# Second layer's attention of a six-layer block on one Trainium2 core: the order of its two branches' pairs, of the weight strips and of the compression

## The reference, cut to what matters

```python
kc = compress(k_cmp, cmp_pe[0], cmp_w1[0], cmp_w2[0])      # gelu(blk @ w1) @ w2, 15 blocks of 32 tokens
vc = compress(v_cmp, cmp_pe[1], cmp_w1[1], cmp_w2[1])
p_c = masked_softmax(s_c, m_c)
o_c = jnp.einsum('bgrqn,bngd->bqgrd', p_c.astype(vc.dtype), vc)
o_s = jnp.einsum('bgrqk,bgqkd->bqgrd', p_s.astype(v_g.dtype), v_g)
o_w = jnp.einsum('bgrqk,bkgd->bqgrd', p_w.astype(vw.dtype), vw)
return gc[..., 0:1] * o_c + gc[..., 1:2] * o_s + gc[..., 2:3] * o_w
```

## Time and profile before

| | us |
|---|---|
| median of 3 runs | 3057.65 |
| lowest, highest | 3055.53, 3057.67 |
| the profiled execution's own time | 3057.54 |
| its span, first to last instruction | 3055.70 |
| mean granted TensorE clock in it | 0.983 of full |

### The profile page before, as it was taken

The page is one execution under the profiler, slowest core; times in us unless marked ns, Lnnn a source line. Parts: engine busy times, 40 slices in busy tenths (PEclk is TensorE's granted clock), DMA queues, the critical chain, the costliest instruction groups (busy, mean ns, idle before and its releaser), DMA issues.

```text
span 3055.7 us, 44834 instructions
## 1 busy us (share of the span) xinstructions
PE 2967.5 (97%) x18942; PEld 2663.0 (87%) x18942; DVE 2128.8 (70%) x2549; ACT 1517.6 (50%) x2040; POOL 39.8 (1%) x30
## 2 busy tenths in 40 slices
PE   9999998999999999999999999999999999999999
PEld 8888997888988899888988989989888898898988
DVE  5677776676657766676877876657778778764776
ACT  5543565434654355534544844545454466454543
POOL 0000000000000000000000000000000000000000
PEclk9999998999999999999999999999999999999999
DMA  7355451354444554355554534535546544352453
GB/s 233 125 166 196 143 177 56 126 196 165 153 138 165 194 169 139 111 197 187 184 196 154 167 127 138 152 104 180 185 165 199 179 152 141 126 165 97 164 195 110
DMA packets 381975, 482.47 MB, mean 158 GB/s; under 512 B 33009, under 2 KB 330143, under 8 KB 381776
## 3 DMA queue, kind: packets, MB, share of 16 engines
q1 hardware_dynamic: 380616, 477.22, 47.5%
q0 software_dynamic: 560, 2.13, 0.2%
q10 hardware_dynamic: 600, 0.27, 0.0%
HBM read 478.47 MB, written 1.08 MB: 157 GB/s over the span
## 4 chain that ended last, share of the span: by engine, by line
PE 85%; DVE 9%; ACT 5%; issue 2%; DMA 0%; DVEq 0%; ACTq 0%
PE ps L425 18%; PE ps L427 17%; PE ps L426 17%; PE ps L464 15%; PE ps L465 7%; DVE wl L408 3%; ACT wh L398 2%; PE ps L463 2%; PE ps L462 1%; PE ps L1377 1%; DVE ar L2689 0%; PE ps L1197 0%; DVE ar L1307 0%; PE ps L714 0%; DVE sm L1312 0%
## 5 line engine op out<-in xcount | busy, mean ns | idle before, releaser
L408 DVE TENSOR_TENSOR wl<-raw,wh 128x2048 fp32r<-128x2048 f32 x456 | 1038.4, 2282 | 424.9 <-ACT wh L398 424.8
L398 ACT ACTIVATE wh<-raw 128x2048 fp32r<-128x2048 f32 x456 | 863.1, 1901 | 479.4 <-PE ps L427 240.2
L464 PE MATMUL ps<-ahl,wh 128*128 128x512 f32 x1904 | 684.0, 398 | 0.0
L425 PE MATMUL ps<-ahl,wh 128*128 128x256 f32 x1928 | 564.5, 293 | 21.6 <-DVE ahl L653 8.7
L426 PE MATMUL ps<-ahl,wh 128*128 128x256 f32 x1928 | 555.0, 288 | 0.0
L427 PE MATMUL ps<-ahl,wl 128*128 128x256 f32 x1928 | 554.5, 288 | 0.0
L465 PE MATMUL ps<-ahl,wl 128*128 128x256 f32 x1904 | 534.7, 281 | 0.0
L464 PEld LDWEIGHTS ps<-ahl,wh 128*128 128x128 f32 x1904 | 358.6, 188 | 76.5
L425 PEld LDWEIGHTS ps<-ahl,wh 128*128 128x128 f32 x1928 | 379.2, 197 | 33.3 <-issue 21.3
L426 PEld LDWEIGHTS ps<-ahl,wh 128*128 128x128 f32 x1928 | 379.7, 197 | 0.3 <-issue 0.2
L427 PEld LDWEIGHTS ps<-ahl,wl 128*128 128x128 f32 x1928 | 379.0, 197 | 0.0
(11 more groups left out here) (409 smaller groups left out, 4087.0 us busy)
## 6 DMA issues: line engine op xcount, KB each, us to landing
raw<-in_ffn_w SPq DMA_DIRECT2D x264, 512.0 KB, 4.2
raw<-in_mlp_w SPq DMA_DIRECT2D x256, 512.0 KB, 4.3
raw<-in_w_in SPq DMA_DIRECT2D x124, 512.0 KB, 4.4
raw<-in_da_w_in SPq DMA_DIRECT2D x48, 512.0 KB, 5.3
raw<-in_ple_gate_w SPq DMA_DIRECT2D x32, 512.0 KB, 4.4
raw<-in_w_ssd_out SPq DMA_DIRECT2D x32, 512.0 KB, 4.3
raw<-in_fox_w_in SPq DMA_DIRECT2D x24, 512.0 KB, 4.6
raw<-in_nsa_w_in SPq DMA_DIRECT2D x20, 512.0 KB, 4.7
```

The source lines that it names most:

```text
L398: nc.scalar.activation(wh[:, slot, 0:sizes[n]], raw[:, slot, 0:sizes[n]], ACT.Copy).then_inc(s_hi, E.adds(s_hi))
L408: nc.vector.tensor_tensor(wl[:, slot, 0:sizes[n]], raw[:, slot, 0:sizes[n]], wh[:, slot, 0:sizes[n]].bitcast(F32), ALU.subtract).then_inc( ...
L425: nc.tensor.matmul(o, wa, xa, start=start, stop=False)
L464: nc.tensor.matmul(o, wa, both, start=start, stop=False)
```

## The change

The 16 pairs go in another order: two of the selected branch, then the same two head pairs of the window branch, and so on by query strips (`nsa_unit`). Window keys are now projected ahead of the loop, window values, queries 1, both compression inputs, queries 2 and queries 3 within turns 0 to 8, by quarters of 12 matmuls before and after a turn's transposes (`NSA_FILL`; all in bank 7, each name waits for the eviction of the one before). Scores are one pair ahead in all turns, each turn does its own values (`deep` is 17 or its default on the other engines, so never used). Gelu moves to turns 6 and 7, the second compression product with all memsets and block copies to turn 9, block scores to 10, mask and sums to 11, block transposes to 12 and 14, products to 13, 14 and 15 (banks 7, 0, 1, 7). Turning the output rows begins after the last values. Values are stored once per group; the block values are copied four times from PSUM, without a copy in SBUF between. Each engine's splits, roundings and loads of strips follow the new order.

```diff
                 else:
-                    dst = orow.rearrange("p q (j c n) -> p c q j n", c=2, n=64)[:, :, :, j % 8, :]
+                    dst = orow.rearrange("p q (j c n) -> p c q j n", c=2, n=64)[:, :, :, unit(j)[0], :]
...
+        NSA_EV = ("q0", "ksel", "gates", "vsel", "kwin", "vwin", "q1", "c0", "c1", "q2", "q3")
+        NSA_FILL = {0: ("vwin", (0, 1), (2, 3)), 1: ("q1", (0,), (1,)), 2: ("q1", (2,), (3,)), 3: ("c0", (0, 1), (2, 3)), 4: ("c1", (0,), (1,)),
+                    5: ("c1", (2,), (3,)), 6: ("q2", (), (0, 1, 2, 3)), 7: ("q3", (0,), (1,)), 8: ("q3", (2,), (3,))}
+        ADDED_BANK = (7, 0, 1, 7)
+
+        def nsa_unit(i):
+
+            return 2 * (i // 4) + i % 2, i % 4 // 2
         nsa_ev = {}
         gah, gal = [view(ar_r, 2048 * v, [P, 16, 60]) for v in range(2)], [view(ar_r, 2048 * v + 1024, [P, 16, 60]) for v in range(2)]
...
+            strip(S)
             for n in range(2):
                 sp_wide(E, d["nsa_cmp_w1"][0, n], 256, 16)
-            for i in range(1, 4):
-                strip(S * i)
-            strip(2048)
-            strip(2304)
+            strip(2 * S)
+            strip(3 * S)
             sp_downs(E, d["nsa_w_out"][0])
...
+
+            def filler(name, part):
+
+
+                if part == 0:
+                    evicted(NSA_EV[NSA_EV.index(name) - 1])
+                    if name == "q2":
+                        E.eng.wait_ge(s_gu, 1)
+                m, h = divmod(part, 2)
+                if name[0] == "c":
+                    n = int(name[1])
+                    if part == 0:
+                        E.eng.wait_ge(s_op, op0 + n + 1)
+                    if h == 0:
+                        held["block"] = pe_block(E, S, DC)
+                    blk, a, b = held["block"]
+                    for k in range(4 * h, 4 * h + 4):
+                        last = mm3(ps[0:60, 7, 0:S], gah[n][:, 8 * m + k], gal[n][:, 8 * m + k], a[:, k, :], b[:, k, :], part == 0 and k == 0, part == 3 and k == DC - 1)
+                    if h:
+                        ends(E, blk, last, s_mm if m else s_wd)
+                    return
+                if part == 0:
+                    held["block"] = pe_block(E, S, DC)
+                blk, a, b = held["block"]
+                c, o = slice(m * P, (m + 1) * P), ps[:, 7, m * S:(m + 1) * S]
+                for k in range(4 * h, 4 * h + 4):
+                    first, stop = part == 0 and k == 0, part == 3 and k == DC - 1
+                    if name[0] == "v":
+                        last = mm3(o, ah[:, k, c], al[:, k, c], a[:, k, :], b[:, k, :], first, stop)
+                    else:
+                        last = mm3(o, a[:, k, c], b[:, k, c], ah[:, k], al[:, k], first, stop)
+                if part == 3:
+                    ends(E, blk, last, s_mm)
 
...
+            E.eng.wait_ge(s_st, E.next(s_st))
+            evicted("gates")
             for j in range(16):
-                if j in (1, 3, 5, 7):
-                    evicted({1: "q1", 3: "q2", 5: "q3", 7: "kwin"}[j])
-                if j < 8:
+                name, before, after = NSA_FILL.get(j, (None, (), ()))
+                if j in (1, 3, 7, 11):
+                    evicted({1: "kwin", 3: "q1", 7: "q2", 11: "q3"}[j])
+                if j < 15:
                     pe_scores(E, score, j + 1, scd)
-                if 7 <= j < 14:
-                    pe_scores(E, score, j + 2, scd)
-                if j in (0, 2, 4, 5, 6):
-                    if j == 4:
-                        E.eng.wait_ge(s_kv, 1)
-                    elif j:
-                        evicted({2: "q1", 5: "q3", 6: "kwin"}[j])
-                    blk = pe_block(E, S, DC)
-                    pe_strip(E, "v" if j == 6 else "q", 7, 0, blk)
-                elif j == 3:
-                    evicted("q2")
+                for part in before:
+                    filler(name, part)
+                if j == 6:
+                    hidden_turned()
+                elif j == 9:
+                    evicted("q3")
                     E.eng.wait_ge(s_gg, 1)
                     compressed()
-                elif j == 7:
-                    evicted("vwin")
+                elif j == 10:
+                    E.eng.wait_ge(s_kv, 1)
                     block_scores()
                 turn(j)
-                if j in (0, 2, 4, 5, 6):
-                    pe_strip(E, "v" if j == 6 else "q", 7, 1, blk, s_km if j == 5 else s_mm)
-                elif j == 15:
-                    E.eng.wait_ge(s_ca, 3)
-                    for b in range(2):
-                        pe_turn_bank(E, b, orow)
-                if j == 0:
-                    evicted("vsel")
-                elif j == 9:
-                    evicted("vwin")
-                if j < 8:
-                    values(j)
-                elif j > 8:
-                    values(j - 1)
-                if j == 10:
+                for part in after:
+                    filler(name, part)
+                if j == 12:
                     E.eng.wait_ge(s_cp, 1)
                     block_turned(0)
-                elif j == 11:
+                elif j == 13:
                     E.eng.wait_ge(s_cc, 1)
-                    E.eng.wait_ge(s_vb, 1)
                     block_values(0)
-                elif j == 12:
+                elif j == 14:
+                    E.eng.wait_ge(s_scd, scd + 15)
+                    block_values(1)
                     E.eng.wait_ge(s_ca, 1)
-                    block_values(1)
-                elif j == 13:
-                    E.eng.wait_ge(s_ca, 2)
                     block_turned(1)
-                elif j == 14:
+                elif j == 15:
...
             for q in range(NT):
-                for r in range(2):
-                    last = nc.scalar.activation(dst[:, q].rearrange("p (g r) n -> p g r n", r=2)[:, :, r, :],
-                                                bank(b)[:, q, :].rearrange("p (g n) -> p g n", g=4), ACT.Copy, scale=r2[:, q:q + 1])
+                last = nc.scalar.activation(dst[:, q], bank(b)[:, q, :].rearrange("p (g n) -> p g n", g=4), ACT.Copy, scale=r2[:, q:q + 1])
...
-                E.eng.wait_ge(s_mm, E.next(s_mm))
-                nc.scalar.activation(gur[n][0:60, :], ps[0:60, 7 - 4 * n, 0:S], ACT.Copy).then_inc(s_ev, E.adds(s_ev))
-                if n == 0:
+
+            def between(j):
+                if j == -1:
+                    E.eng.wait_ge(s_kd, E.next(s_kd))
+                    act_keys(E, 1, 7)
                     act_hi(E)
-            E.eng.wait_ge(s_gur, 1)
-            nc.scalar.activation(gu, ps[:, 5, 0:240].rearrange("p (v m n) -> p v m n", v=2, m=2), ACT.Copy).then_inc(s_gu, 1)
-
-            def between(j):
-                if j in (0, 2, 4):
-                    i = j // 2 + 1
+                elif j == 0:
+                    E.eng.wait_ge(s_mm, E.next(s_mm))
+                    act_values(E, vwin, 7)
+                    act_hi(E)
+                elif j in (2, 6, 8):
+                    i = {2: 1, 6: 2, 8: 3}[j]
                     E.eng.wait_ge(s_mm, E.next(s_mm))
                     nc.scalar.activation(qk[:, 2 * i:2 * i + 2, 0, :], bank(7), ACT.Copy).then_inc(s_ev, E.adds(s_ev))
-                elif j == 1:
-                    E.eng.wait_ge(s_gz, 1)
-                    nc.scalar.activation(ge, gz, ACT.Exp, scale=-2.0 * math.sqrt(2.0 / math.pi)).then_inc(s_gx, 1)
-                elif j == 5:
-                    E.eng.wait_ge(s_kd, E.next(s_kd))
-                    act_keys(E, 1, 7)
-                elif j == 6:
+                    act_hi(E)
+                    if j == 6:
+                        E.eng.wait_ge(s_gz, 1)
+                        nc.scalar.activation(ge, gz, ACT.Exp, scale=-2.0 * math.sqrt(2.0 / math.pi)).then_inc(s_gx, 1)
+                elif j in (3, 5):
                     E.eng.wait_ge(s_mm, E.next(s_mm))
-                    act_values(E, vwin, 7)
-                elif j == 9:
+                    nc.scalar.activation(gur[j // 5][0:60, :], ps[0:60, 7, 0:S], ACT.Copy).then_inc(s_ev, E.adds(s_ev))
+                    act_hi(E)
+                    if j == 3:
+                        act_hi(E)
+                    else:
+                        E.eng.wait_ge(s_gur, 1)
+                        nc.scalar.activation(gu, ps[:, 7, 0:240].rearrange("p (v m n) -> p v m n", v=2, m=2), ACT.Copy).then_inc(s_gu, 1)
+                elif j == 4:
+                    act_hi(E)
+                elif j == 10:
                     E.eng.wait_ge(s_cm, 1)
                     nc.scalar.activation(pc[:, :, :, 0:NCMP], pc[:, :, :, 0:NCMP], ACT.Exp).then_inc(s_cx, 1)
-                elif j in (10, 13):
-                    E.eng.wait_ge(s_ct, {10: 1, 13: 2}[j])
+                elif j in (12, 14):
+                    E.eng.wait_ge(s_ct, {12: 1, 14: 2}[j])
                     nc.scalar.activation(pcT, ps[:, 7, :].rearrange("p (g n) -> p g n", g=4), ACT.Copy).then_inc(s_cc, 1)
-                if j < 7:
-                    act_hi(E)
```

(81 more changed lines are left out.)

38 lines of the change are left out of this document (14 added, 24 removed).

## The result

The changed kernel takes 3063.14 us, the median of 19 runs (3057.93 to 3067.31), beside 3057.04 for the kernel before in the same number (3052.95 to 3062.17). The ratio is 1.0017, 95% interval 1.0011 to 1.0023: **slower, by 3 to 7 us**, about the 0.2% that the prediction set as its bound. The forecast was 3064.7. The profiled execution has a span of 3064.66 us, 8.9 over the 3055.73 of before, where the medians are 6.1 apart; so terms read from it come out somewhat larger than the medians' difference. In one of the later sets one execution of the kernel before took 12423 us and one of a variant 7409 us; the ratios leave them out, the medians move by at most 0.6 us with them.

A forecast was written before the change was run, and what follows sets the result against it. TensorE bounds the kernel, busy 97% of the span, with waits and low clock in the second layer's attention. From 3057.5, +4.6 us at full clock and +2.6 for the clock gave 3064.7; own range 3061 to 3069, wider 3054 to 3072.

The forecast's parts named there:

- The keys' wait: Before the window values' strip, sharing bank 7: TensorE waits 4.1 us for ScalarE's copies of the window keys.
- the walk: Hand-stepped engine orders through the second layer's attention at full clock: end 531.3, waits 24.1 us, +4.6 us.
- Values 5 and 8: Filled turns: two splits in turn 4 leave a 1.5 us wait, split and gelu in turn 7 one of 2.1.
- The wait before the block scores: After turn 9: a weight split, memsets and copies on VectorE make TensorE wait 3.6 us.
- The ring: Bare pairs 9 to 15: values wait for output behind scaling behind newer scores; 5.3 or 5.7 us a pair, not 4.15.
- bare value groups 5.2 to 6 us apart: Sign of being right, in pairs without weight strips: that spacing, each group released by VectorE's stored output.
- The clock term: Attention stretch: 30 us at 1.2 GHz, costing 11.4 us instead of 8.8, so +2.6 us.
- the end of 45: Upper end for the attention stretch's time at 1.2 GHz: 45 us, costing 8.3 more than now.
- slower by over 0.2%: Whole time: slower by more than 6.1 us, chance 0.45, beside 0.44 for within that bound.
- Interleaving pays: Rival at the bare pairs: the ring does not close, -8.6 us, 3049; chance 0.13.
- the block branch's chain: VectorE's turn 9 memsets and copies before block scores; if done before pair 9, another 3.6 us less.
- the third rival: Clock stays down through all bare pairs: ring at 1.2 GHz, 45 us, 4.6 + 8.3, 3070.4; chance 0.12.

The follow-up runs named there:

- the run with held matmuls: Changed kernel plus 130 extra matmuls with unread results in TensorE's waits before the window values' strip, before block scores and after some transposes: 3059.64 us, ratio 1.0007.
- the run with three edits: Changed kernel with VectorE storing outputs before scaling from turn 1, turn 9's split after the copies, window keys in bank 6: 3040.47 us (0.9950); third set 3047.78 (0.9960).
- the two later sets: The changed kernel without edits, measured again against the kernel before: 3064.94 us (ratio 1.0029) and 3066.69 us (1.0034).
- the last experiment: Three edits (outputs first, late split, keys in bank 6) plus seven extra unread matmuls in each of turns 9 to 11: 3040.80 us, ratio 0.9950 to the kernel before.

## Why the prediction was right

*Terms that held.* The matrix work did not change, and nothing outside the stretch did: the stretch's 9.0 us are the whole difference of the two profiled executions. The keys' wait was put at 4.1 and measured 3.67, released by the copies named, with every hand-over of its chain within 0.2 us (keys' copies from 419.0 by the walk, 418.94 measured). Values 5 and 8: 1.5 and 2.1 against 1.25 and 1.73. Values 8 were put at 484.6 at full clock; they came at 487.5, after 6.8 us at 1.2 GHz. In the sum for these turns the nine transposes stood at 0.71 us each, where rows 3 give 0.9; between quarters the changed kernel's trace has 0.57. The wait before the block scores: 3.6 against 3.14, by the VectorE copies named. The ring: values 11 to 14 released by VectorE's stored output, and open once the order was changed; values 10 waited for ScalarE's copy instead, where the prediction had VectorE for every bare group. The sign "bare value groups 5.2 to 6 us apart" failed as it was written: they were 8.0, 8.0, 6.5 and 5.6 apart, since the walk was at full clock and these turns were not. At full clock, in the run with held matmuls, the last three distances are 6.0, 5.5 and 5.6, and that is the ring as walked. Waits in all: 24.1 at full clock, 18.9 measured with slow matmuls covering part, as 19.5 and 15.0 for the kernel before.

*The clock term, the step that was mis-sized.* "I expect 30 us at 1.2 GHz: 11.4 instead of 8.8, +2.6 us." The 30 leave out the low clock before 410. Counted in the same way, the changed kernel has 38 us (2 x 0.14 x 134.5 from 410 on), halfway from 30 to the end of 45 that the prediction kept for its worst case. The walk ends at 531.3 and the measured stretch at 544.5, so these 38 us cost 13.2, or 0.35 each: +4.4 over the 8.8 of the old order and not +2.6. The amount was too low, and the price of 0.38 was about right. Two other readings of the price lie on either side. The held matmuls gave 0.30. Between executions of one and the same kernel, 32 of the kernel before in the first set of the experiments, the time falls by some 2.4 us for each 0.001 by which the mean clock rises, that is 0.39 for each us at 1.2 GHz (0.001 of 3057 us is 6.1 us at the low clock). It is no constant: it depends on how much of the slow work falls where TensorE would wait anyway, and the run with three edits in the second set had 17 us more of it behind 410 than the one with held matmuls, for a stretch only 2.0 us longer (there the extra matmuls may have taken time of their own). The block scores alone, taken at 3.6 us for full clock, ran for 7.0 us at 1.2 GHz.

*The size.* The walk and the clock term gave +7.2; the 19 runs give a ratio worth +5.2 (3 to 7 by the interval), the two later sets +8 and +10. The forecast was "slower by over 0.2%" as the likelier of two nearly equal cases; the 19 runs put it just inside the bound. Which of the two it is for this kernel, a spread of 10 us between executions does not settle. That the forecast of 3064.7 lies within 2 us of all three medians is in part luck: the waits were sized well, but the clock term was 1.8 too small, and the sets themselves differ by 4.

*The rivals.* Interleaving pays was wrong for this kernel as written, since the ring closed, and right in its potential: it had been priced at -8.6 us from opening the ring and clearing the block branch's chain, and the version with these two and the keys' bank runs 10 to 16 us under the kernel before. How much of that lead is the interleaving itself is not shown. The change also stores the values once instead of twice and moves the copies of the block branch, and the old order was not run with its own late outputs opened in turns 8 to 15. The rule of the Trainium skill (Perfetto Trace Analysis, Optimization Strategy), that interleaving regimes may improve performance, is borne out here only by the versions in which the order inside the turn was changed as well. The copies from PSUM took 0.415 us each, as the row said, and not twice the SBUF copy. The clock stayed low through most of the bare pairs (0.58 from 512 to 525), which was the third rival's mechanism, without reaching its price. The Trainium skill (TensorE: Matmul & The Clock Gate, A second HAM failure mode) has short idles between matmul groups as what makes the clock swing; the last experiment's trace agrees, with three idles of 0.9 us filled and a clock of 1.00 in place of 0.68 and 0.60, in one profiled execution against two.

## What to carry to other kernels

When a pipelined loop is rearranged so that every turn does its own last step, write down for each in-order engine what stands in front of the result that the next turn waits for. Here a finished output stood behind a scaling that needed newer scores, and this closed a ring of one turn; swapping two operations on VectorE, with no work removed, was worth 6 to 7 us. A strip that is to cover a wait must not share its bank with the one whose eviction is waited for. And a rearrangement that comes out level or slightly worse may still be the better start: in turns 1 to 7 the old order had nothing to gain from the same edit, the new one with three edits went 0.4 to 0.5% below it.

## What the runs showed of the hardware

Seven extra matmuls of 256 columns in each of three waits of 0.9 us came with a granted clock of 1.00 from 485 on, where it had been 0.68 and 0.60 from 485 to 512 in the two profiles without them; the stretch was 2.0 and 4.5 us shorter with more work in it. Of the whole time this is not shown: the medians are 3040.8 with them, 3040.5 and 3047.8 without. The block scores, 32 narrow matmuls of 30 columns in 3.8 us, did not bring the clock down by themselves in that run; in both profiles without the extra matmuls the clock fell at them or right behind them.

The spread between executions of one kernel follows the clock, and a good part of it lies outside the attention. Of 32 executions of the kernel before in one set, from 3051.1 to 3062.2 us, those with a mean granted clock of 0.981 take 3061 to 3062 and those with 0.985 take 3051. The two profiles of the kernel with three edits differ by 9.1 us. The stretch has 17 us at the low clock in one and 24 in the other, which makes 2.5 of the 9.1; the other 6.6 lie behind the projection, where the code is the same. Why the clock falls in one execution and not in another was not tested.
